# First two units and the gates on x before its norm, with the scaled x transposed a second time

## The reference, cut to what matters

```python
SEQ, D_MODEL = 256, 2048

def _rmsnorm(x, w=None):
    xf = x.astype(jnp.float32)
    y = xf * lax.rsqrt(jnp.mean(xf * xf, axis=-1, keepdims=True) + NORM_EPS)
    return y if w is None else y * w.astype(jnp.float32)

def _hybrid_layer(h, norm_w, w_in, ...):
    u = _rmsnorm(h, norm_w)
    proj = jnp.matmul(u, w_in.astype(jnp.float32))
    ...split into ml_q, ml_k, ml_v, ml_o, ml_z, ml_i, ml_f, dn_qkv, dn_z, dn_b, dn_a, gate_a, gate_b
    i_pre = _softcap(ml_i + ml_i_bias)...          # the "gates": 48 narrow columns of w_in
    h_a = _mlstm_chunkwise(...)
    qkv = _causal_conv_silu(dn_qkv, dn_conv_w)     # 6144 columns: the twelve qkv units
    h_b = _gated_delta_chunkwise(_l2norm(q), _l2norm(k), v, beta, g)
    ...
```

## Time and profile before

| | us |
|---|---|
| median of 3 runs | 1906.93 |
| the runs | 1906.93, 1910.53, 1906.90 |
| the profiled execution | 1906.96 |
| its span | 1905.2 |
| TensorE busy in the span | 1885.3 |
| first product starts | 15.64 |

### The profile page before, as it was taken

How to read it: one execution, slowest core, us unless ns; L and a number is a source line. 1 busy time by engine, 2 the same in 40 slices (tenths; PEclk the granted TensorE clock), 3 DMA queues, 4 the chain that set the end, 5 groups by cost and what they waited for, 6 DMA issues and landing times.

```text
span 1905.2 us, 27734 instructions
## 1 busy us (share of the span) xinstructions
PE 1885.3 (99%) x10964; PEld 1635.8 (86%) x10964; DVE 1407.6 (74%) x2068; ACT 911.0 (48%) x1394; POOL 328.5 (17%) x550
## 2 busy tenths in 40 slices
PE   8999999999999999999999999999999999999998
PEld 8999999878888989888888888888888888888886
DVE  5786877767989788889989667666464676657675
ACT  6546455445433433434445465554444455544544
POOL 1034425161212222313223100000000000111000
PEclk9999999999999999999999999999999999999999
DMA  8555454546788787777888857655656543544563
GB/s 263 149 159 177 124 176 144 155 155 194 263 271 288 255 270 238 238 261 248 288 293 307 297 188 233 232 177 186 196 169 203 175 133 126 185 147 150 186 224 132
DMA packets 209745, 393.17 MB, mean 206 GB/s; under 512 B 13000, under 2 KB 62448, under 8 KB 208208
## 3 DMA queue, kind: packets, MB, share of 16 engines
q1 hardware_dynamic: 191248, 323.17, 52.0%
q0 software_dynamic: 18224, 68.17, 11.2%
q10 hardware_dynamic: 144, 0.07, 0.0%
HBM read 387.13 MB, written 4.23 MB: 205 GB/s over the span
## 4 chain that ended last, share of the span: by engine, by line
PE 92%; DVE 4%; POOL 1%; ACT 1%; issue 1%; DMA 0%; SPq 0%; DVEq 0%; ACTq 0%; POOLq 0%
PE GB L2188 50%; PE GB L2215 19%; PE GB L2200 9%; PE GB L2203 5%; PE SB L419 1%; PE SB L1759 1%; DVE WL L2112 1%; PE SB L1751 1%; POOL TB L1122 1%; POOL XB L1125 1%; PE SB L1858 1%; PE SB L1865 1%; PE SB L829 1%; PE SB L1216 1%; ACT WH L2107 0%
## 5 line engine op out<-in xcount | busy, mean ns | idle before, releaser
L2112 DVE TENSOR_TENSOR WL<-raw,WH 128x1024 fp32r<-128x1024 f32 x605 | 730.9, 1235 | 180.3 <-ACT WH L2107 179.1
L2107 ACT ACTIVATE WH<-raw 128x1024 fp32r<-128x1024 f32 x605 | 622.7, 1059 | 312.2 <-PE GB L2188 226.2
L2188 PE MATMUL GB<-WH,uHL 128*128 128x512 f32 x1792 | 484.6, 392 | 1.2 <-DVE WL L2112 1.2
L2188 PEld LDWEIGHTS GB<-WH,uHL 128*128 128x128 f32 x1792 | 333.2, 188 | 69.2 <-issue 1.3
L2215 PE MATMUL GB<-uHL,WH 128*128 128x256 f32 x2048 | 291.4, 285 | 1.6 <-DVE uHL L455 1.6
L2188 PE MATMUL GB<-WH,hHL 128*128 128x512 f32 x1024 | 279.4, 395 | 0.0
L2188 PE MATMUL GB<-WL,uHL 128*128 128x512 f32 x896 | 276.1, 389 | 0.0
L2215 PEld LDWEIGHTS GB<-uHL,WH 128*128 128x128 f32 x2048 | 264.0, 192 | 2.9 <-DVE uHL L455 1.8
L2188 PEld LDWEIGHTS GB<-WH,hHL 128*128 128x128 f32 x1024 | 190.6, 188 | 41.1 <-issue 2.7
L1446 DVE SCALAR_TENSOR_TENSOR macc<-wm,csil,macc 128x512 f32<-128x512 f32 x300 | 209.5, 748 | 2.7 <-DMA wm<-in_w_mod 1.5
L2188 PEld LDWEIGHTS GB<-WL,uHL 128*128 128x128 f32 x896 | 168.2, 188 | 35.5
(11 more groups left out here) (408 smaller groups left out, 1911.9 us busy)
## 6 DMA issues: line engine op xcount, KB each, us to landing
raw<-in_w_in SPq DMA_DIRECT2D x512, 512.0 KB, 4.5
raw<-in_w_out SPq DMA_DIRECT2D x96, 512.0 KB, 5.2
wm<-in_w_mod POOLq DMA_DIRECT2D x64, 512.0 KB, 5.5
wm<-in_w_mod POOLq DMA_DIRECT2D x64, 256.0 KB, 4.3
xin<-in_x SPq DMA_DIRECT2D x4, 512.0 KB, 5.8
E<-decay_rows POOLq DMA_DIRECT2D x4, 512.0 KB, 4.2
hres<-in_x POOLq DMA_DIRECT2D x1, 2048.0 KB, 10.7
cin<-in_ctx POOLq DMA_DIRECT2D x1, 2048.0 KB, 11.5
```

The lines of the kernel that those rows point to most:

```text
L2107: e.activation(place(s)[0][:, :, :], raw[s % NR][:, :, :], ACT.Copy).then_inc(*wh.inc("WH", s))
L2112: e.tensor_tensor(low[:, :, :], raw[s % NR][:, :, :], f32(high[:, :, :]), sub).then_inc(*wl.inc("WL", s))
L2188: m = e.matmul(banks[j][:, :], x[:, c, 128 * j:128 * j + 128], w[:, k, :], start=i == 0 and k == 0 and n == 0, stop=i == 7 and k == 1 and ...
```

## The change

1. **Start.** x is loaded in eight column pieces of 256 KB between the first five weight tiles instead of four pieces of 512 KB ahead of them (`FIRST_X`). The norm weight's 16 columns are loaded first and by themselves, on ScalarE's queue; the rest of `vcol` follows there. `busy_pe` issues 8 matmuls instead of 30 and waits only for `ones`; `idle_pe` adds 6 after the first transposes. The first transposes read the unscaled x. Slot 0 is done by a new function in three groups of eight matmuls, with the transposes of pair 1 between the second and the third.
2. **Units 0 and 1 and the gates use x * norm weight without rstd.** Sums of squares (ScalarE, slots 2 to 5), root and reciprocal (slots 5.5 and 6), then one matmul of ones by diag(rstd) in the middle of slot 7 that puts rstd as a row in every partition, copied to `rrow`. `scaled_dve` multiplies the finished unit 0 (behind slot 7) and unit 1 (behind slot 15) by that row into `zz`, 4 VectorE instructions of 128x256 each; the convolution reads `zz`. The gates' result is multiplied by `rrow` on VectorE instead of being copied by ScalarE.
3. **u is made again for unit 2 on.** ScalarE scales the whole of `xin` (four instructions, slots 8 to 9.5), and eight more pairs are transposed and written over `uHL` (stage "u2", slots 10 to 15.5). ScalarE writes pair k only after slot 8 + k; slot 16 + k waits for the low half of pair k.
4. The squares' sums of the queries move three slots later. GpSimd loads its constants later. The whole-x scaling ahead of the first transposes is gone from both engines.

```diff
+RAW = 2
-CONVS = (1, 2, 3, 4, 5, 6, 7.5, 9, 10, 10.5)
+NXA, NXD, NXP = (2, 3, 4, 5, 6, 7, 8, 8.5, 9, 9.5), (5.5, 6), (6.5,)
+CONVS = (1, 2, 3, 4, 5, 6, 7.5, 12, 13, 13.5)
...
+    at("nxa", 0, NXA)
+    at("nxd", 0, NXD)
+    at("nxp", 0, NXP)
+    at("u2", 0, (10, 11, 12, 13, 13.5, 14, 14.5, 15.5))
...
+            e.wait_ge(*g_pe.at("g"))
+            e.wait_ge(*nx_act.at("row"))
+            e.tensor_tensor(r(SS), SB[0][:, 0:256], rrow[:, :], mul).then_inc(*g_dve.inc("c"))
...
+        def norm_pe(e, bank):
+            e.wait_ge(*nx_dve.at("diag"))
+            claim(e, bank, 2, nx_act.at("row"))
+            m = e.matmul(SB[2][:, 0:256], ones[:, :], junk[:, 0:256], start=True, stop=True, skip_group_check=True)
...
+        def scaled_dve(e, r, banks):
+            e.wait_ge(*slot.at("mm", end("qkv", r)))
+            e.wait_ge(*nx_act.at("row"))
+            for j in range(4):
+                v = e.tensor_tensor(zz[:, j, :], half(banks[j // 2], j % 2), rrow[:, :], mul)
+            v.then_inc(*z_dve.inc("z", r))
...
+            if (unit.kind, unit.n) == ("qkv", RAW):
+                e.wait_ge(*tr_dve.at("l", TU2 + i))
...
+        def first_pe(e, banks, stages):
+            wh_, wl_ = place(0)
+            for said, x, w in ((tr_act.at("h", TU), uH, wh_), (tr_dve.at("l", TU), uL, wh_), (wl.at("WL", 0), uH, wl_)):
+                if w is wh_:
+                    e.wait_ge(*wh.at("WH", 0))
+                else:
+                    next(stages["u"])
+                e.wait_ge(*said)
...
+        FIRST_X = {0: (0,), 1: (1, 2), 2: (3,), 3: (4, 5), 4: (6, 7)}
...
-            take_turns(stages, -1)
-            scaled_dve(e, "c")
+            next(stages["u"])
+            split_dve(e, 0)
+            next(stages["u"])
+            e.wait_ge(vcol_in, 16)
```

More of the change, by code:

```diff
@@ L422, in turn_pe, with turn_act @@
                 yield
-        def turn_act(e, base, H, pairs, scale, shift, *free):
+        def turn_act(e, base, H, pairs, scale, shift, *free, freed=None):
             for k in range(pairs):
@@ L483, in gates_pe @@
             e.wait_ge(*tr_dve.at("l", TU + 7))
-            claim(e, bank, 0, g_act.at("c"))
+            claim(e, bank, 0, g_dve.at("c"))
             for k in range(KT):
@@ L655, in norm_act @@
         def norm_act(e):
[L656 to L661 removed]
+            for j in range(2):
+                for i in range(2):
+                    n = 2 * j + i
+                    for p in range(4):
+                        e.wait_ge(x_in[4 * j + p], 16)
@@ L677, in busy_pe @@
-        def busy_pe(e):
-            for said, n in ((init.at("ones"), 15), ((x_in[2], 16), 5), ((x_in[3], 16), 6), (nx_dve.at("ss"), 4)):
-                e.wait_ge(*said)
-                for _ in range(n):
-                    e.matmul(SB[3][:, 0:128], ones[:, :], ones[:, :], start=True, stop=True, skip_group_check=True)
+            yield
+            e.wait_ge(*nx_pe.at("row"))
+            e.activation(rrow[:, :], SB[2][:, 0:256], ACT.Copy).then_inc(*nx_act.inc("row"))
+            yield
@@ L684, in norm_dve @@
+            e.wait_ge(*tr_pe.at("t", TU + 7))
+            for j in range(2):
+                for i in range(2):
+                    c = slice(1024 * j, 1024 * j + 1024)
+                    e.activation(xin[:, i, c], xin[:, i, c], ACT.Copy, scale=st[:, 4 + i:5 + i]).then_inc(*nx_act.inc(f"x{2 * j + i}"))
+                    yield
         def norm_dve(e):
@@ L688, in norm_dve, with busy_pe, idle_pe @@
             e.tensor_scalar(rs[:, 0:2], st[:, 4:6], 1.0 / D, 1e-6, mul, add).then_inc(*nx_dve.inc("var"))
+            yield
             newton_dve(e, nx_dve, st[:, 4:6], rs[:, 0:2], rs[:, 2:4], nx_act.at("sqrt"))
             e.wait_ge(*nx_dve.at("rstd"))
+            for i in range(2):
+                v = e.tensor_scalar(junk[:, 128 * i:128 * i + 128], ident[:, :], st[:, 4 + i:5 + i], None, mul)
+            v.then_inc(*nx_dve.inc("diag"))
+            yield
+        def norm_pe(e, bank):
+            e.wait_ge(*nx_dve.at("diag"))
+            claim(e, bank, 2, nx_act.at("row"))
+            m = e.matmul(SB[2][:, 0:256], ones[:, :], junk[:, 0:256], start=True, stop=True, skip_group_check=True)
+            m.then_inc(*nx_pe.inc("row"))
+            yield
+        def busy_pe(e):
+            e.wait_ge(*init.at("ones"))
+            for _ in range(8):
+                e.matmul(SB[3][:, 0:128], ones[:, :], ones[:, :], start=True, stop=True, skip_group_check=True)
+        def idle_pe(e):
+            for _ in range(6):
+                e.matmul(SB[3][:, 0:128], ones[:, :], ones[:, :], start=True, stop=True, skip_group_check=True)
         cond_act = steps("cond_act", "e")
@@ L2172, in product_pe @@
             else:
-                m = channels_pe(e, unit, s, banks, stages)
+                m = channels_pe(e, unit, s, banks, stages) if s else first_pe(e, banks, stages)
             m.then_inc(*slot.inc("mm", s))
@@ L2204, in halves_pe @@
                                  skip_group_check=True)
+            return m
+        def first_pe(e, banks, stages):
[6 more added lines that the diff above has]
+                e.wait_ge(*said)
+                for k in range(2):
+                    for j in range(4):
+                        m = e.matmul(half(banks[j // 2], j % 2), w[:, k, 128 * j:128 * j + 128], x[:, k, :],
+                                     start=x is uH and w is wh_ and k == 0 and j % 2 == 0, stop=False, skip_group_check=True)
             return m
@@ L2259, in product_dve @@
             banks = pair(u)
+            if k == "qkv" and n < RAW:
+                scaled_dve(e, n, banks)
             if k in ("qkv", "gb", "ya", "ga"):
@@ L2422, in _ @@
             e.wait_ge(ident_in, 16)
-            stages = {"u": turn_pe(e, bank, TU, xin, 8, {
-                k: (nx_dve.at("x0" + c), nx_act.at("x1" + c)) for k, c in ((0, "a"), (2, "b"), (4, "c"))}), "gates": gates_pe(e, bank),
+            stages = {"u": turn_pe(e, bank, TU, xin, 8, {k: ((x_in[k], 16),) for k in range(8)}),
+                      "u2": turn_pe(e, bank, TU2, xin, 8, {0: (nx_act.at("x1"),), 4: (nx_act.at("x3"),)}),
+                      "nxp": norm_pe(e, bank), "gates": gates_pe(e, bank),
                       "hb": turn_pe(e, bank, THB, OB, 8, {0: (dz_dve.at("b1", 3),)}),
@@ L2435, in _ @@
             stages.update({("ml", hf): ml_pe(e, bank, hf) for hf in range(2)})
-            take_turns(stages, -1)
+            next(stages["u"])
+            idle_pe(e)
             for s in range(NS):
```

92 lines of the change are left out of this document (42 added, 50 removed).

## The result

The changed kernel takes 1913.74 us in the median of 8 runs (1912.58 to 1916.37), the kernel before 1907.13 beside it (8 runs, 1906.90 to 1910.53). The ratio is 1.0032 with a 95% interval of 1.0023 to 1.0041, so it is slower by 0.3%, some 6.6 us. The profiled execution took 1913.21, with a span of 1911.4 against 1905.2. Three single executions of those made for this document lay far off (3146.82, 9176.01 and 9997.73 us); the ratios and their intervals leave them out.

What follows compares the result with a forecast made beforehand. TensorE, busy 1885.3 us and almost never waiting outside the start, was taken as the bound. Terms: -4.6 + 3.8 + 1.2 + 0.9 + 2.1 + 1.4 = +4.8 us on 1906.96; forecast kept at 1911.6, range 1906.3 to 1915.0.

Steps and rivals of the forecast that it cites:

- Term 1: Start of the kernel: slot 1 begins at 14.3 instead of 18.97, a gain of 4.6 us (range 3.4 to 5.6).
- Term 2: TensorE's added work: eight second pairs of transposes 3.5 us and the rstd matmul 0.33, together +3.8 us.
- Term 3: Middle of slot 7: TensorE waits for the identity scaled by rstd, +1.2 us.
- term 4: Behind slot 12: TensorE's gates' transposes wait for bank SB1, held by pair 1 of the second set, +0.9 us.
- term 5: Slot 19: TensorE waits for VectorE's late split, +2.1 us (range 0.5 to 3.7).
- Term 6: Tail of VectorE's lag: slot 24 waits 0.5, the score products about 0.9 more, +1.4 us (range 0 to 2.5).
- VectorE keeping up: Rival: VectorE's chain from slot 12 to 19 is 2.1 us shorter, slot 19 and tail waits vanish: 1908.2 us, chance 0.27.
- The start paying for all: Rival: slot 1 at 13.4 and no later waits, so faster than before, 1904.8 us; chance 0.06.

Runs made afterwards that it cites:

- the kernel with the row later: Changed kernel with rstd's row matmul half a slot later, behind slot 7 instead of in its middle: 1912.55 us, ratio 1.0023.
- the bank experiment: Changed kernel with the gates' two small transposes in bank SB3 instead of SB1: 1914.01 us, ratio 1.0028.
- the doubled scaling: Changed kernel with unit one's scaling done a second time, four more VectorE instructions behind slot 15: 1913.65 us, ratio 1.0031.
- the experiment with small low halves: Changed kernel with the second transposes' low halves written only 8 of 256 columns wide, leaving out VectorE work: 1909.90 us, ratio 1.0011.
- all mends: Changed kernel with ten idle matmuls, rstd's row later, small transposes in SB3, tanh behind next split, exponents behind two splits: 1903.95 us, ratio 0.9978.
- the kernel with the tanh alone: Changed kernel with ScalarE's tanh of each convolution behind the next weight split instead of ahead of it: 1906.76 us, ratio 0.9994.

## Why the prediction was right, and where it was off

Forecast 1911.6 with a range of 1906.3 to 1915.0, measured 1913.74: inside, on the forecast side (slower), 2.1 us above. By the profiled executions +6.25 stands against +4.8 (which makes 1911.8 from 1906.96, 0.2 above the number that was kept).

| term | predicted | measured | |
|---|---|---|---|
| 1 start | -4.6 | -4.11 | slot 1 at 13.53, not 14.3, but at a low clock |
| 2 TensorE's work | +3.8 | +4.15 | pairs 3.47, rstd's matmul 0.68 instead of 0.33 |
| 3 wait in slot 7 | +1.2 | +1.05 | right |
| 4 wait for SB1 | +0.9 | +1.03 | right in the trace, no loss of its own (SB3) |
| 5 slot 19 | +2.1 | +1.53 | right in kind |
| 6 tail | +1.4 | +2.46 | slot 24 0.57, products 1.89 |

- **Term 1.** The half pace was put into slot 0 at 0.7. Slot 0 ran at full pace (16 matmuls in 2.18) and slot 1, after the 1.91 us wait, at 0.64 of the clock, for 1.50. The Trainium skill, "TensorE: Matmul & The Clock Gate", Part 1, says that the low rate is the default and that the count of slow matmuls varies from run to run. The nine profiles with this start and no idle matmuls agree in that: slot 1 was slow from its first matmul in two, from its middle in one, and at full pace in six. The identity landed 3.3 us after its issue and the norm weight after 4.5, at 5.78, 0.3 earlier than assumed. The fit of the Trainium skill that the prediction quotes for these two loads is given there for DMAs that GpSimd issues; they went out on ScalarE's queue, and 3.3 and 4.5 are above the 2.0 to 2.2 that it would give.
- **Term 2.** The rstd matmul was priced by rows of 128 columns without its gaps. It was mis-sized by 0.35, of which 0.10 is the matmul: in the kernel with the row later, where nothing waits for it, it costs 0.43 (0.24 until the next product, 0.19 within that). The other 0.25 came with the wait.
- **Terms 3 to 5.** Each chain was summed from rows of before, and each wait was found where it was put, within 0.6, with the releaser that was named. Two small slips are in the sums: term 4's chains are 0.8 apart (7.9 - 7.1), not 0.9, and 26 instructions at 0.05 make term 5's range 0.8 to 3.4, not 0.5 to 3.7. What was wrong is the word "sum". Term 3 is a loss of its own: without its wait of 1.05 the products came 1.06 earlier. But the wait of term 4, taken away in the bank experiment, came back at slot 19 (1.03 became 1.06), and of what the doubled scaling and the low clock added at slot 19 (2.8) the products showed 0.92.
- **Term 6** is the step that failed in size, 1.06 too small. The prediction said that mask and exponents come later relative to TensorE, but carried VectorE's lag on without looking at the decay rows' way out to memory and back. In the trace of before VectorE waited 2.30 us for TensorE there, which hid it. The transfer of `E` took 4.4 us then and 6.8 now, with the weight loads beside it; that is 0.90 of the 6.11 by which the mask was late. The Trainium skill, "DMA: Bandwidth & Descriptors", Anatomy of one DMA, would give an estimate of 3.2 for its 512 KB; the profiles have 4.4 to 8.0, so the measurement decides: the fit is too low here.
- **The rivals.** VectorE keeping up was given 0.27: the experiment with small low halves builds that case and lands at 1909.9, where 1908.2 was worked out; its profile has a wait of 4.10 at the products, 2.08 of it because the transfer of `E` took 8.0 us, and a low clock behind it. The start paying for all was given 0.06, "no case below 1903": with all mends the changed kernel reaches 1903.95, by an order that neither the change nor the prediction touched.

Left open: what makes the transfer of `E` take 4.4 or 8.0 us. When the weight loads are issued does not explain it alone. Counted from the issue of `E`, they go out at -3.80, +2.01 and +4.57 us (within 0.01) in eight kernels whose transfer took 6.1 to 8.0; in the five that took 4.4 to 5.2 the last one before it stands elsewhere, between -6.0 and -1.6, and the two behind it at the same +2.0 and +4.6. The change's parts were also not each put alone on the kernel before; the sums' and loads' later places rest on the trace, in which nothing waits for them.

## What to carry to other kernels

When a lead between two engines is used up, its waits are stops on the way to one appointment; find the last one (here the mask, 12.65 to 12.67 us ahead of the products in eleven kernels of fourteen) before pricing those on the way, and try a mend at the first of them against the last. Look at what an engine does while it is the late one: VectorE, short of time, stood idle for 2.07 us twice, since the engine that feeds it had put work that depended on VectorE ahead of work that did not. With the tanh behind the split the changed kernel was 5.3 us faster by the profiled executions and 7.0 by the medians, and the idle time could be seen in the trace of before. The same pattern spoiled a mend: moving VectorE's scaling later made ScalarE's copy wait, and with it the splits behind the copy and VectorE itself (1.93).

## What the runs showed of the chip

- TensorE's clock fell to its low level after some of the longer waits, in some executions and not in others. Ahead of the decayed products the profiles have waits of 2.21, 2.45, 2.49, 2.59 and 4.10 followed by slow products (1.72 to 2.05 for two matmuls that take 1.10), but 2.54 and 2.93 followed by full pace; after 1.10 to 1.33 it did not fall (five kernels). Ahead of slot 19 a wait of 2.76 was followed by a slow slot and one of 2.50 by full pace. A wait of 0.49 was followed by a slow slot in two kernels (1.70 and 1.74 for 1.20), right behind the query sums, 16 matmuls of one column each. One fall costs 1.4 to 2.1 us here.
- Ten idle matmuls inside a wait of 1.91 us left slot 1 at full clock in all three kernels that had them (as it was in six of the nine without), and the best version's eleven times lie within 0.73 us, those of the kernel with the tanh alone within 2.14.
- The same transfer of 512 KB on GpSimd's queue took between 4.4 and 8.0 us over fourteen kernels (4.4, 4.5, 4.5, 4.9, 5.2, six between 6.0 and 6.5, 6.8, 7.3, 8.0), issued at 99.7 to 109.7 us beside the weight loads.
